# State-space decays from running sums on all partitions, a gate slot in the last stick-breaking pair, and the attention's root chain in the first round

## What is computed

```python
def hybrid_mixer(u, w_in, conv_w, conv_b, dt_bias, a_log, d_skip, ssd_norm_g, attn_norm_g, w_out):
    q, k, v, z, xs, bm, cm, dt_raw = split(u @ w_in)
    o_att = rmsnorm(stick_breaking_attention(q, k, v), attn_norm_g)   # 16 heads of 64, causal
    xs, bm, cm = split(silu(causal_conv4(concat(xs, bm, cm)) + conv_b))
    dt = softplus(dt_raw + dt_bias)
    a = -exp(a_log)
    y = ssd_chunked(xs, dt, a, bm, cm)      # 16 heads of 64, 2 groups, state 128, chunks of 128
    y = (y + d_skip * xs) * silu(z)
    y = rmsnorm(y in 2 groups, ssd_norm_g)
    return concat(o_att, y) @ w_out
```

## Time and profile before

| | us |
|---|---|
| median of three runs | 2018.39 |
| the runs | 2016.9 to 2018.68 |
| the profiled execution | 2017.63 |
| its span | 2015.9 |
| PE busy | 1967.8 (98%) |
| DVE busy | 1136.9 (56%) |
| ACT busy | 828.9 (41%) |
| POOL busy | 111.3 (6%) |

### The profile page before, as it was taken

One profiled execution on the slowest core, in us unless ns is written; L12 is line 12 of the kernel. 1 busy time (PEld: TensorE's weight loads), 2 busy tenths in 40 slices (PEclk: granted clock), 3 DMA queues, 4 the chain that ended last, 5 costly groups with the idle time before them and its releaser, 6 DMA issues.

```text
span 2015.9 us, 25890 instructions
## 1 busy us (share of the span) xinstructions
PE 1967.8 (98%) x10430; PEld 1599.1 (79%) x10430; DVE 1136.9 (56%) x1853; ACT 828.9 (41%) x1412; POOL 111.3 (6%) x131
## 2 busy tenths in 40 slices
PE   8999999999999999999999999999999999999997
PEld 6767767888888888888877777888888788888886
DVE  5567765744465444422738888795555465444323
ACT  4155532533353232322437777454434453323221
POOL 0000000000020000000200001331110020000000
PEclk9999999999999999999999999999999999999999
DMA  7111121333323333333322221113234223333331
GB/s 277 57 34 51 53 63 54 89 88 99 100 63 107 94 94 94 95 89 87 96 74 63 63 64 53 53 42 96 83 105 126 74 77 94 95 95 94 91 97 61
DMA packets 49432, 170.56 MB, mean 85 GB/s; under 512 B 5520, under 2 KB 8080, under 8 KB 48928
## 3 DMA queue, kind: packets, MB, share of 16 engines
q1 hardware_dynamic: 48816, 166.73, 27.7%
q0 software_dynamic: 496, 2.16, 0.3%
HBM read 166.77 MB, written 2.10 MB: 84 GB/s over the span
## 4 chain that ended last, share of the span: by engine, by line
PE 92%; DVE 6%; issue 1%; ACT 1%; DMA 0%; SPq 0%; DVEq 0%
PE acc L1796 58%; PE bank L1796 18%; PE bank L1885 2%; PE bank L2096 1%; PE acc L2300 1%; PE bank L1958 1%; PE bank L2131 1%; PE bank L2033 1%; DVE bank L1158 1%; PE bank L1931 1%; DVE w_lo L1078 1%; PE bank L2287 1%; PE bank L2321 1%; DVE residual L1164 1%; PE bank L1818 1%
## 5 line engine op out<-in xcount | busy, mean ns | idle before, releaser
L1078 DVE TENSOR_TENSOR w_lo<-w_raw,w_hi 128x1024 fp32r<-128x1024 f32 (+2 forms) x306 | 365.9, 1198 | 303.6 <-ACT w_hi L592 303.1
L1796 PE MATMUL acc<-act_hi,w_hi 128*128 128x512 f32 (+1 forms) x1160 | 457.2, 394 | 17.3 <-DVE w_lo L1078 9.5
L1796 PE MATMUL acc<-act_hi,w_lo 128*128 128x512 f32 (+1 forms) x1160 | 445.0, 384 | 0.0
L1796 PE MATMUL acc<-act_lo,w_hi 128*128 128x512 f32 (+1 forms) x1160 | 445.0, 384 | 0.0
L592 ACT ACTIVATE w_hi<-w_raw 128x1024 fp32r<-128x1024 f32 (+2 forms) x306 | 314.5, 1029 | 210.8 <-PE acc L1796 180.9
L1796 PEld LDWEIGHTS acc<-act_hi,w_hi 128*128 128x128 f32 x1160 | 218.6, 188 | 71.5 <-issue 16.4
L1796 PEld LDWEIGHTS acc<-act_hi,w_lo 128*128 128x128 f32 x1160 | 218.7, 189 | 46.9
L1796 PEld LDWEIGHTS acc<-act_lo,w_hi 128*128 128x128 f32 x1160 | 218.9, 189 | 45.8 <-issue 2.2
L1796 PE MATMUL bank<-act_hi,w_hi 128*128 128x512 f32 (+1 forms) x520 | 192.6, 370 | 1.2 <-DVE w_lo L1078 1.2
L1796 PE MATMUL bank<-act_lo,w_hi 128*128 128x512 f32 (+1 forms) x520 | 191.0, 367 | 0.0
L1796 PE MATMUL bank<-act_hi,w_lo 128*128 128x512 f32 (+1 forms) x520 | 190.9, 367 | 0.0
(11 more groups left out here) (451 smaller groups left out, 3042.6 us busy)
## 6 DMA issues: line engine op xcount, KB each, us to landing
w_raw<-w_all SPq DMA_DIRECT2D x282, 512.0 KB, 3.5
w_raw<-w_all SPq DMA_DIRECT2D x16, 384.0 KB, 3.1
residual<-xT SPq DMA_DIRECT2D x8, 256.0 KB, 7.4
cmp_w_k<-w1k SPq DMA_DIRECT2D x1, 2048.0 KB, 8.5
cmp_w_v<-w1v SPq DMA_DIRECT2D x1, 2048.0 KB, 12.7
w_raw<-w_all SPq DMA_DIRECT2D x8, 256.0 KB, 2.7
out_t<-residual SPq DMA_DIRECT2D x16, 128.0 KB, 1.7
ret_decay<-decay POOLq DMA_DIRECT2D x4, 256.0 KB, 3.4
```

Source lines behind the costliest of these rows:

```text
L1078: TT(WL[:, c % RAW_RING, 0:nb * P], WR[:, c % RAW_RING, 0:nb * P], WH[:, c % HI_RING, 0:nb * P].bitcast(F32), ALU.subtract).then_inc(s_lo, 1)
L1796: ins = MM(bank[:, cols], w[:, at, k * P:(k + 1) * P], x, start=first and r == 0 and k == 0, stop=last and r == 2 and k == nb - 1)
```

## The change

The decays inside a chunk no longer come from segment operands. `decay_sums` multiplies the column of a * dt of one chunk and head, broadcast to 128 columns, with `upper_incl`, so that each of 128 partitions holds A[t] in banks 1 and 2. ScalarE then forms max(A[j] - A[t], 0) by a Relu for each chunk and head, with scale -1 and A[j] as bias from a new small tile `a_dt_sums` (made once by one more matmul and copy behind the dt sums), and takes exp of its negative in SBUF. The row decays exp(A[t]) are read from the same two banks, 64 partitions from each. The matmuls into bank 3 (L2207), GpSimd's `segments` and the semaphores for them are gone.

The rest is order. Slot 0 of `ssd_z` is multiplied in four parts: k 0 and 1, 2 and 3, and 4 behind the first three turned blocks of the last pair, k 5 to 7 behind the turn of the B tiles. `decay_sums(0)` moves to the front of the opening. The attention's row sums come just before round 0, its reciprocal and spread (into bank 3) behind the states of round 0, its copy on ScalarE in front of `decay_exps(1)`. In the rounds, a slot's k 0 to 5 come before the new states and k 6 and 7 between the masked products and L2248. VectorE makes the attention products one earlier or later in places (a5 moves to round 4, a7 to round 5), and the SSD products of rounds 6 and 7 behind the states. On ScalarE the last four conv silus move behind the copies of the B tiles, and the first weight roundings and the root move around `decay_exps(0)`.

```diff
--- before.py
+++ after.py
@@ -110,6 +110,7 @@
 MIX = MIX_FIRST + list(itertools.chain.from_iterable(MIX_TURNS))
 MIX_AT = {name: j for j, name in enumerate(MIX)}
+LAST_PAIR = {0: range(0, 2), 1: range(2, 4), 2: range(4, 5)}
...
@@ -121,7 +122,7 @@
     return p * len(SB_ORDER) + SB_ORDER.index((what, b)) + 1
 
 
-MIXER = {1: ["a0", "a1"], 2: ["a2", "a3"], 3: ["a4", "a5"], 4: ["a6", "a7"], 6: ["s0", "s1"], 7: ["s2", "s3"],
+MIXER = {1: ["a0", "a1"], 2: ["a2", "a3"], 3: ["a4"], 4: ["a5", "a6"], 5: ["a7"], 6: ["s0", "s1"], 7: ["s2", "s3"],
          8: ["s4", "s5", "s6", "s7"]}
 MIXER_AT = {name: j for j, name in enumerate(itertools.chain.from_iterable(MIXER[n] for n in sorted(MIXER)))}
 
@@ -140,6 +141,7 @@
 START += [(s, (k,)) for k in range(5, DK) for s in range(TOGETHER)]
 
 
+BEFORE_STATES = 6
...
@@ -323,7 +325,7 @@
         NROWS = EV[:, 3, :]
         X1 = place("ssd_x_dt", [P, SC, 2, SSD_P], 48)
         X2 = place("ssd_x_decayed", [P, SC, 2, SSD_P], 50)
-        LSG = place("ssd_segments", [P, SC, 2, P], 52)
+        ACS = place("a_dt_sums", [P, SC, SSD_HEADS], 127)
         LM = place("ssd_decays", [P, 2, SC, P], 104)
         ATTN_RS, SSD_RS = EV[:, 2, :], EV[:, 3, :]
         STT_ = place("ssd_states", [P, 3, P], 110)
...
@@ -531,15 +530,6 @@
             for p in range(SB_PAIRS - 1):
                 attn_square(p)
 
-            def segments(n):
-
-                heads = slice(n * 2, n * 2 + 2)
-                wait_apart(pool, sem("ssd_rows"), n + 1, sem("pool_seen"))
-                for c in range(SC):
-                    nc.gpsimd.tensor_tensor(LSG[:, c], const("later").unsqueeze(1).broadcast_to([P, 2, P]),
-                                            ADT[:, c, heads].unsqueeze(2).broadcast_to([P, 2, P]), ALU.mult).then_inc(
-                        sem("ssd_lhs"), 1)
-
             def ssd_square(n):
 
                 wait_apart(pool, s_ysq, n + 1, sem("pool_seen"))
...
@@ -871,6 +857,7 @@
                     A(DTL[:], DTL[:], ACT.Ln, bias=1.0).then_inc(sem("dt_log"), 1)
             act.wait_ge(sem("dt_sums"), 1)
             A(DEND[:], PS[5][:, 0:64].rearrange("p (c h) -> p c h", c=SC), ACT.Exp)
+            A(ACS[:], PS[5][:, 128:192].rearrange("p (c h) -> p c h", c=SC), ACT.Copy)
             A(CDEC[:], PS[5][:, 64:128].rearrange("p (c h) -> p c h", c=SC), ACT.Exp).then_inc(sem("dt_decays"), 1)
 
             def sb_abs(p, b):
@@ -941,31 +928,37 @@
             act.wait_ge(sem("sb_pv"), SB_PAIRS)
             A(OSB[:, SB_PAIRS - 1, :], PS[5][:], ACT.Copy).then_inc(sem("sb_out"), 1)
             out_square(SB_PAIRS - 1)
-            for t in range(4, CONV_TILES):
+            for t in range(4, DK):
                 conv_silu(t)
             for g in range(2):
                 act.wait_ge(sem("ssd_bt"), g + 1)
                 A(BTK[:, g], PS[3 + g][:].rearrange("p (c n) -> p c n", c=SC), ACT.Copy).then_inc(sem("ssd_b_tokens"), 1)
+            for t in range(DK, CONV_TILES):
+                conv_silu(t)
 
             def z_silu(t):
                 act.wait_ge(s_acc, TILE0["ssd_z"] + t + 1)
                 A(ZS[:, t, :], ZS[:, t, :], ACT.Silu).then_inc(sem("z_silu"), 1)
-            z_silu(0)
-            row_root("attn", 1)
             split_hi(nxt)
             nxt += 1
-            act.wait_ge(s_spread, ROWS["attn"] + 1)
-            A(ATTN_RS, PS[2][:], ACT.Copy).then_inc(sem("mixer_rstd"), 1)
-            split_hi(nxt)
-            nxt += 1
+            z_silu(0)
 
             def decay_exps(n):
+
                 act.wait_ge(sem("ssd_seg"), n + 1)
                 for hh in range(2):
-                    A(LM[:, hh], PS[1 + hh][:].rearrange("p (c t) -> p c t", c=SC), ACT.Exp).then_inc(sem("ssd_seg_exp"), 1)
-                act.wait_ge(sem("ssd_rows"), n + 2)
+                    for c in range(SC):
+                        ins = A(LM[:, hh, c, :], PS[1 + hh][:, c * P:(c + 1) * P], ACT.Relu, scale=-1.0,
+                                bias=ACS[:, c, 2 * n + hh:2 * n + hh + 1])
+                    ins.then_inc(sem("ssd_fall"), 1)
+                for hh in range(2):
+                    act.wait_ge(sem("ssd_fall"), 2 * n + hh + 1)
+                    A(LM[:, hh], LM[:, hh], ACT.Exp, scale=-1.0).then_inc(sem("ssd_seg_exp"), 1)
                 act.wait_ge(sem("ssd_done"), max(n, 1))
-                A(row_exp(n)[:, P:S], PS[3][:, P:S], ACT.Exp).then_inc(sem("ssd_row_exp"), 1)
+                for hh in range(2):
+                    half = slice(DH * hh, DH * (hh + 1))
+                    ins = A(row_exp(n)[half, P:S], PS[1 + hh][half, P:S], ACT.Exp)
+                ins.then_inc(sem("ssd_row_exp"), 1)
 
             def y_square(n):
                 act.wait_ge(sem("ssd_done"), n + 2)
@@ -977,7 +970,11 @@
                 k = int(name[1])
                 product_hi(PROD0["mixer"] + MIXER_AT[name], sb_hi(k) if name[0] == "a" else YSH[k // 4][:, k % 4, :])
 
+            act.wait_ge(sem("dt_decays"), 1)
             decay_exps(0)
+            split_hi(nxt)
+            nxt += 1
+            row_root("attn", 3)
             for n in range(8):
                 if n:
                     y_square(n - 1)
@@ -990,6 +987,9 @@
                     mixer_hi(name)
                 split_hi(nxt)
                 nxt += 1
+                if n == 0:
+                    act.wait_ge(s_spread, ROWS["attn"] + 1)
+                    A(ATTN_RS, PS[3][:], ACT.Copy).then_inc(sem("mixer_rstd"), 1)
                 if n < 7:
                     decay_exps(n + 1)
                 for u in {0: (1, 2), 2: (3, 4), 4: (5, 6), 5: (7,)}.get(n, ()):
@@ -1631,12 +1631,9 @@
                 dve.wait_ge(sem("ssd_cb_psum"), g + 1)
                 V.tensor_copy(CBM[:, g], PS[(5, 0)[g]][:].rearrange("p (c t) -> p c t", c=SC)).then_inc(sem("ssd_cb"), 1)
             rescale("ssd_z", 0, ZS[:, 0, :])
-            row_rstd("attn")
             split_lo(nxt)
             nxt += 1
             rescale("ssd_z", 1, ZS[:, 1, :])
-            split_lo(nxt)
-            nxt += 1
 
             def by_head(t, n, c0, c1, width):
 
@@ -1679,15 +1676,15 @@
                 for hh in range(2):
                     dve.wait_ge(sem("ssd_seg_exp"), n * 2 + hh + 1)
                     TT(LM[:, hh], LM[:, hh], CBM[:, n // 4], ALU.mult).then_inc(sem("ssd_m"), 1)
+                if n == 0:
+                    split_lo(nxt)
+                    nxt += 1
                 if n == 1:
                     dve.wait_ge(sem("mixer_rstd"), 1)
-                if n == 5:
-                    row_rstd("ssd0")
-                if n == 6:
-                    dve.wait_ge(sem("mixer_rstd"), 2)
                 names = MIXER.get(n, ())
-                for name in names:
-                    mixer_product(name, ATTN_RS if name[0] == "a" else SSD_RS)
+                if n < 6:
+                    for name in names:
+                        mixer_product(name, ATTN_RS)
 
                 dve.wait_ge(sem("ssd_new"), n + 1)
                 chain.link(V.tensor_copy(STT_[:, 0, :], PS[4][:, 0:P]))
@@ -1700,6 +1697,15 @@
                         chain.link(ins)
                     else:
                         ins.then_inc(sem("ssd_states"), 1)
+                if n == 0:
+                    row_rstd("attn")
+                if n == 5:
+                    row_rstd("ssd0")
+                if n == 6:
+                    dve.wait_ge(sem("mixer_rstd"), 2)
+                if n >= 6:
+                    for name in names:
+                        mixer_product(name, SSD_RS)
                 for name in names:
                     mixer_low(name)
                 if n < 6:
@@ -2077,6 +2083,7 @@
                 if s == 11:
                     pe.wait_ge(sem("adt"), 1)
                     MM(PS[5][:, 0:64], const("later"), ADT[:].rearrange("p c h -> p (c h)"), start=True, stop=True)
+                    MM(PS[5][:, 128:192], const("upper_incl"), ADT[:].rearrange("p c h -> p (c h)"), start=True, stop=True)
                     MM(PS[5][:, 64:128], ones, ADT[:].rearrange("p c h -> p (c h)"), start=True, stop=True).then_inc(
                         sem("dt_sums"), 1)
             after_boundary(1, "ffn1_down", "sb_qkv", dt_steps)
@@ -2149,6 +2156,8 @@
                 more = p + 1 < SB_PAIRS
                 for b in range(5):
                     turned(p, b)
+                    if not more and b in LAST_PAIR:
+                        gemm("ssd_z", 0, HH, HL, ks=LAST_PAIR[b])
                 pe.wait_ge(sem("sb_early_t"), p * 2 + 2)
                 if more:
                     qkv_ready(p + 1, "qk")
@@ -2172,66 +2181,54 @@
                     mixed(MIX_TURNS[p][2:])
 
 
-            gemm("ssd_z", 0, HH, HL)
+            def decay_sums(n):
+
+                if n:
+                    pe.wait_ge(sem("ssd_row_exp"), n)
+                for hh in range(2):
+                    for c in range(SC):
+                        ins = MM(PS[1 + hh][:, c * P:(c + 1) * P],
```

(60 more changed lines are left out.)

5 lines of the change are left out of this document (removed).

## The result

The changed kernel takes 2007.07 us (median of 5 runs, 2004.52 to 2007.57), beside 2018.03 us for the kernel before on the same chip (2016.01 to 2018.68). The ratio is 0.9945, with a 95% interval of 0.9934 to 0.9956: faster by 11 us, 0.55%. The profiled execution took 2005.59 us with a span of 2003.4; before it was 2017.63 and 2015.9, so 12.0 and 12.5 less. The forecast was 2006.0 for the median and 2005.2 for the profiled execution, 12.4 us less in both.

The account below looks back on a forecast made before the run. TensorE was taken as the bound (92% of the last-ending chain). Opening and round 0 give 7.5 us, rounds 5.3, the end -0.4: together 12.4, so 2005.2 profiled and 2006.0 us median; range 2002.0 to 2011.0.

Parts of the forecast that it names:

- (a): Last pair in the opening: 15 gemm matmuls moved between turned blocks save net 3.4 us, cover intact.
- (b): Value products after the last pair: filled idle gaps keep TensorE's clock up, recovering 1.4 us (bounds 0 and 1.4).
- (c): Rest of the opening: row matmuls save 0.8 us, small waits 0.7, the attention spread 0.9, given back behind round 0.
- Rounds, TensorE: Round 0's end to round 7's: TensorE's work is 10.69 us a round, 77.4 in all, against 86.0 before.
- Rounds, waiting: Time over TensorE's floor in the rounds: 1.9 us from VectorE and 1.4 us from ScalarE.
- ScalarE's part: Exp load between Relus and exps delays masks: 0.3 us in each of five rounds, 1.4 us in all.
- Rounds, VectorE: GpSimd's relief cuts VectorE's 12.36 us rounds to 11.36, masks still beside squares; 1.9 us over the floor remain.
- The end: Behind round 7: VectorE's last product starts about 1 us later after L2248, so 0.4 us is lost.
- R1: Rival: ScalarE and VectorE both fit, rounds come to half a us over the floor, 2003.2 us; chance 0.16.
- R2: Rival: VectorE or ScalarE replaces TensorE as bound in the rounds, giving back about 4.5 us, 2010.5; chance 0.18.
- R3: Rival: clock falls all the same, or the fill delays the pair's end; 1.4 us less gain, 2007.4; chance 0.10.
- R4: Rival, slower: ScalarE becomes the bound if a Relu takes 0.61 us or more; 2022 at 0.7; chance 0.04.

Follow-up runs that it names:

- e2: Changed kernel, the 15 fill matmuls kept between the turned blocks but thrown away, slot 0 of ssd_z multiplied whole afterwards: 2010.71 us, ratio 0.9962.
- e3: Kernel before the change, with only the fill of the last pair added: 2019.24 us, ratio 1.0009.
- e1: Changed kernel without the fill: slot 0 of ssd_z in one piece behind the turn of the B tiles: 2011.11 us, ratio 0.9964.
- e10: Changed kernel with the attention's root chain (row sums, root, reciprocal, spread) back in the opening: 2006.26 us, ratio 0.9938.
- e4: Changed kernel with every gemm slot of the rounds multiplied whole ahead of the new states: 2008.94 us, ratio 0.9955.
- e7: Changed kernel with one 512-column Relu per head instead of four of 128, so some decays differ from the reference: 2005.02 us, ratio 0.9935.
- e6: Changed kernel with the silu of the last z tile moved one round later on ScalarE: 2005.31 us, ratio 0.9941.
- e8: Changed kernel with GpSimd's four segment products per round put back, their result unused: 2005.67 us, ratio 0.9942.
- e12: Changed kernel with both GpSimd's segment products and the six row matmuls put back: 2010.13 us, ratio 0.9962.
- e9: Changed kernel with the six row matmuls of rounds 1 to 7 put back, their result overwritten: 2009.52 us, ratio 0.9955.
- e11: Changed kernel with a one-column Exp ahead of each round's Relus and the last z silu one round later: 2005.87 us, ratio 0.9938.

## Why the prediction was right, step by step

**(a) The fill: right.** 3.4 us forecast, 3.50 measured (e2 against the changed kernel). "Cover intact" was right only for the changed kernel as a whole. The forecast named the weights and the bank that the fill needs, and not the chain that the 15 matmuls had covered: e3 is the fill without the rest of the change, and loses 1.1 us in the stretch.

**(b) The clock: right,** 1.4 forecast, 1.32 measured (e1 against e2). Against the kernel before itself the value products are 1.67 shorter (2.40 for 4.07); I had put them at 2.65 without the fall.

**(c) The rest of the opening: right in sum.** Round 0 ends 7.86 us earlier, 7.5 forecast; less the 4.82 of the fill, 3.04 remain for the rows, the root chain, the small waits and the cut, where I had 2.7. The parts do not add: the root chain alone is 3.05 (e10) and the cut 0.45 (e4; 0.3 forecast).

**Rounds, TensorE: the floor was 2.2 us too high.** I added 10.69 us partly from durations, which overlap from one matmul to the next. A round without waits is 10.37 us (rounds 1 of e10 and 4 of e7), and 11.25 with row sums or spread: four times 10.37 and three times 11.25 are 75.2, not 77.4. Start to start, round 1 of e10 is 0.66 (L2249), 1.79, 0.36 (turn), 5.78 (gemm), 0.76 (new states) and 1.02 (masked products); I had 0.94, 1.79, 0.59, 5.60, 0.68 and 1.09. In the rows above, L2249 has 0.83 and 0.67 to the next start.

**Rounds, waiting: 2.6 us too low.** 81.12 - 75.2 = 5.9 us over this floor, 4.3 of them waits that TensorE's rows name, where I had 3.3 (1.9 VectorE, 1.4 ScalarE). So the 80.7 forecast for 81.12 is right partly because two errors cancel. The size of ScalarE's part stood well: the Relu was 0.25 (0.26 forecast), eight took 2.18 (2.2), the load stood where I put it, and taking it off the path gives 1.61 (1.4). What was wrong is the place. I spread it evenly over five rounds; it comes in rounds 1, 2 and 7. And two causes that I had at 0.3 a round or nothing are most of the 5.9. The root chain in round 0 costs 2.5 in rounds 1 and 2 (e10); apart from the loads I had called it free, because TensorE waits for nothing at its spread. The last silu costs 1.8 in round 7 (e6).

**Rounds, VectorE: mechanism right, victim and worth wrong.** I expected the masks to stay slow beside the squares (11.36 us a round). They ran in 1.29 in every round; the products took the collision, in round 2 (2.42) and round 6 (2.00). And of the steps that ended the 12.36 us rounds, GpSimd's relief is 1.1 to 1.5 us (e8, e12), the row matmuls 3.8 (e9).

**Round 7: missed.** The largest single wait, 1.62 us, comes from the last silu and its load ahead of the copy that round 7 waits for. The forecast counted ScalarE's work per round (10.6 of 10.7 us) but did not follow the order of its queue there.

**The end: 0.4 lost forecast, none found** (12.83 against 12.81), but the cover has no more than 0.2 us left: the last squares end at 1359.90 and the row sums start at 1360.12. e4, e6 and e11 show what lies behind it, e6 and e11 with 1.1 us of a new collision added.

**The rivals.** R1 (2003.2) put the rounds at 77.9 us together, R2 (2010.5) at 85.2: 81.1 excludes both. R3 is out by the clock of 1.00 and e2. R4 is out by the Relu at 0.25 (its last figure was too low in any case: 0.09 more on eight Relus in seven rounds over 2019 is 2024, not 2022).

## What to carry to other kernels

Work moved into an idle gap has two prices: it fills the gap, and it is gone as cover from where it stood; look there for the chain that it hid before you count the gain. When a stretch gets shorter by a microsecond, look at the next place where TensorE meets another engine, and at what the other engines' instructions now run beside: there the gain can come back as a wait, and the wait can cost the clock as well, as the 1.83 us of e6 did. A function moved on an engine with tables also moves the load behind it: the root between two exponentials put a load into round 1. Sum start to start, not durations, for a floor of TensorE.

## What the runs showed of the hardware that I had not expected

- **A wait of about a microsecond can cost TensorE's clock behind it, or not.** 0.89 us of waiting in e6 was followed by windows at 0.67 and 0.50 and cost 1.8 us more; 1.62 us in the changed kernel was followed by 1.00, and the same 1.62 in e2 by 0.57 and 0.58. In e4 the runs lie in two groups, 2006.35 and 2006.84, and 2011.03 and 2011.11 us, with mean clocks of 0.996 and 0.993; only one of the four has a trace, so where they differ is not shown.
- **VectorE's product on two SBUF operands and GpSimd's sum of squares.** A pair of products takes 1.41 us alone and 2.42 beside one GpSimd instruction of 1.34 that began 0.13 earlier; the surplus, 1.0, is nearly the 1.2 us that this instruction still had to run. The Trainium skill (SBUF — State Buffer, SBUF: two separate sides) says that the shared ports are locked for a whole instruction and the other engine blocks meanwhile; these rows agree with that. Which VectorE instruction pays changed with what ran then: masks before, products now, masks again in round 2 of e8. GpSimd can pay as well: in round 4 of the changed kernel the products start at 1315.95 and take 1.41, and GpSimd's sum starts at 1316.93 and takes 1.59 instead of 1.27 to 1.34. Where both start within 0.01 us (round 7 of e6), the products take 2.52.
- **Most table loads between data and its reader cost nothing here.** Six of the eight rounds load the Exp table between Relus and exponentials, 7.7 us in all; pulling the loads ahead of the Relus gives 1.61 us.
